# Norm, routing, plan and shared gate and up in one stage, and branch products on rounded halves, in a 3-layer float32 program

## What is computed

```python
# first block: three branches, each 512 wide, weighted by gates
proj = jnp.einsum('btnm,nmd->btnd', branches, w_branch[l])
gates = jax.nn.sigmoid(cols['merge']).reshape(b, t, N_BRANCH, D_MODEL)
x = x + (gates * proj).sum(axis=2) @ w_out[l]
...
# second block, each of 2 layers: two branches, then norm, modulation, experts
y = jax.nn.sigmoid(gate_a) * (o_a @ w_branch_a) + jax.nn.sigmoid(gate_b) * (o_b @ w_branch_b)
return y @ w_out
...
x = layer_norm(ALPHA * x + gate1 * y, ln1_g[l], ln1_b[l])
h = x * (1 + scale2) + shift2
y = moe_ffn(h, ...)
...
# moe_ffn: 64 experts in 8 groups; 4 groups, then 8 experts a token
scores = jax.nn.sigmoid((xt @ router_w).astype(jnp.float32))
...
shared = (jax.nn.silu(xt @ ws_gate) * (xt @ ws_up)) @ ws_down
return (routed + shared).reshape(B, S, D)
```

## Time and profile before

| | us |
|---|---|
| median of 3 runs | 3909.67 |
| lowest and highest | 3906.97, 3912.04 |
| the profiled execution | 3907.32 |
| its span, first to last instruction | 3905.2 |
| TensorE busy | 3391.9 (87%) |
| VectorE busy | 1570.4 (40%) |
| ScalarE busy | 942.6 (24%) |

### The profile page before, as it was taken

How to read it: one execution, slowest core, us unless ns; L and a number is a source line. 1 busy time by engine, 2 the same in 40 slices (tenths; PEclk the granted TensorE clock), 3 DMA queues, 4 the chain that set the end, 5 groups by cost and what they waited for, 6 DMA issues and landing times. The chain is left out here.

```text
span 3905.2 us, 47770 instructions
## 1 busy us (share of the span) xinstructions
PE 3391.9 (87%) x14923; PEld 2112.4 (54%) x14924; DVE 1570.4 (40%) x3950; ACT 942.6 (24%) x1993; POOL 200.1 (5%) x204
## 2 busy tenths in 40 slices
PE   3887887997999888997799999958899779999985
...
GB/s 122 79 21 28 44 79 39 177 143 140 134 195 134 93 137 23 70 39 54 285 407 400 406 395 402 369 175 129 23 68 41 54 282 415 402 400 392 391 289 194
DMA packets 287126, 748.55 MB, mean 192 GB/s; under 512 B 25883, under 2 KB 167581, under 8 KB 230788
## 3 DMA queue, kind: packets, MB, share of 16 engines
...
...
## 5 line engine op out<-in xcount | busy, mean ns | idle before, releaser
L2502 PE MATMUL up_ps<-experts,x_turned 128*64 128x512 f32 (+1 forms) x2256 | 699.0, 623 | 22.7 <-DMA experts<-in_w_up_dram 21.2
L2502 PEld LDWEIGHTS up_ps<-experts,x_turned 128*64 128x64 f32 (+1 forms) x2256 | 261.4, 161 | 383.2 <-issue 382.6
L257 DVE TENSOR_TENSOR pieces_lo<-weights,pieces_hi 128x512 fp32r<-128x512 f32 (+1 forms) x412 | 274.1, 682 | 314.4 <-ACT pieces_hi L251 313.1
L251 ACT CAST pieces_hi<-weights 128x512 fp32r<-128x512 f32 (+1 forms) x412 | 244.8, 613 | 452.9 <-PE banks L269 93.5
L2526 PE MATMUL y_ps<-experts,hid_turned 128*64 128x512 f32 (+1 forms) x1128 | 345.6, 601 | 1.6 <-ACT hid_turned L2583 1.6
L2661 DVE TENSOR_TENSOR hid_seats<-up_ps,gated 128x256 f32<-128x256 f32 x94 | 57.5, 612 | 607.4 <-ACT gated L2576 607.4
L267 PE MATMUL gate_ps<-h_hi,pieces_hi 128*128 128x512 f32 x624 | 262.4, 420 | 37.8 <-DVE pieces_lo L257 32.0
L267 PE MATMUL products<-h_hi,pieces_hi 128*128 128x512 f32 x464 | 195.4, 421 | 65.5 <-DVE pieces_lo L257 65.5
L269 PE MATMUL gate_ps<-h_hi,pieces_lo 128*128 128x512 f32 x624 | 247.0, 396 | 0.0
L268 PE MATMUL gate_ps<-h_lo,pieces_hi 128*128 128x512 f32 x624 | 246.8, 396 | 0.0
L2526 PEld LDWEIGHTS y_ps<-experts,hid_turned 128*64 128x64 f32 (+1 forms) x1128 | 117.5, 154 | 222.2 <-issue 222.2
...
## 6 DMA issues: line engine op xcount, KB each, us to landing
...
```

Source lines behind the costliest of these rows:

```text
L251: act.copy(self.like(view, self.hi[:, i % self.BUFFERS, :, :]), view).then_inc(s["hi_ready"], 1)
L257: dve.tensor_tensor(lo, view, hi.bitcast(F32), ALU.subtract).then_inc(s["lo_ready"], 1)
L2502: made = pe.matmul(up_ps[part, b, :].rearrange("p (h n) -> p h n", h=2), xT[:, b, k, part], experts.up(b + i)[:, :, k, :], start=(k == 0), ...
```

## The change

1. **Merges.** The branch outputs are rounded and split too, into the two halves' buffers that y uses later and a new pair for the last branch, and the branch product is made like the others, as a third piece of its unit (12 instructions in place of 4 in float32). Units now go branch by branch, the column tiles inside; the sums of all 8 tiles are kept where the first branches' outputs were. A chunk holds one unit, and VectorE frees it when it has split the third piece; the waits for `branch_made` go. The first block's ring has 3 slots of 32 x 128 columns instead of 36 x 128.
2. **One stage, `route_tokens`,** in place of the norm, modulation, transposes, `route` and `make_lists`. The norm works in rows: x is transposed to rows of tokens, VectorE takes mean and variance of each row, ScalarE normalises while it empties the bank, and the tiles are transposed back, where ScalarE applies gain and shift times ALPHA. The modulation makes h, from which rows of tokens are made for the gathers after the router's product. The shared gate and up products have their own weights buffer and stand around the counts and the plan. SyncE loads the first experts' weights (`first_loads`) as soon as the plan stands, still in this stage.
3. **The shared down product** moves into `routed_experts`, between the first searches for seats and the first turn; ScalarE copies its banks to `acc` first.
4. **Tables.** The gather table (40 + 640 columns in place of 1320) and the rotation table are loaded in every layer, and TensorE waits only for the gather table. The zeros are set by GpSimd in each layer.

The core of the diff:

```diff
-    for m in range(DK):
-        add("merge", *[w[:, :, C_MERGE + b * D + m * P:C_MERGE + b * D + (m + 1) * P] for b in range(3)],
-            *[rows(wb[b], 4)[:, :, m * P:(m + 1) * P] for b in range(3)])
+    for b in range(3):
+        for m in range(DK):
+            add("merge", w[:, :, C_MERGE + b * D + m * P:C_MERGE + b * D + (m + 1) * P],
+                rows(wb[b], 4)[:, :, m * P:(m + 1) * P])
...
         pieces = []
         for i in range(n):
-            c = c0 + i // n_branch
-            wm = ring.slot(c, DK, P, i % n_branch * DK * P)
-            pieces += [(c, wm[:, 0:4, :], False), (c, wm[:, 4:8, :], False)]
+            wm = ring.slot(c0 + i, DK, P)
+            pieces += [(c0 + i, wm[:, 0:4, :], False), (c0 + i, wm[:, 4:8, :], False),
+                       (c0 + i, ring.slot(c0 + i, 4, P, DK * P), True)]
...
                 for i in range(n):
-                    m, b = i // n_branch, i % n_branch
-                    wb = ring.slot(c0 + m, 4, P, n_branch * DK * P + b * 4 * P)
...
                         pe.wait_ge(s["gate_ready"], i - 1)
-                    split.product(pe, s, 2 * i, gate_ps[:, i % 2, :], h_hi, h_lo, 0, True, False)
-                    split.product(pe, s, 2 * i + 1, gate_ps[:, i % 2, :], h_hi, h_lo, 4, False, True)
-                    if b == 0:
-                        ring.wait(pe, c0 + m)
+                    split.product(pe, s, 3 * i, gate_ps[:, i % 2, :], h_hi, h_lo, 0, True, False)
+                    split.product(pe, s, 3 * i + 1, gate_ps[:, i % 2, :], h_hi, h_lo, 4, False, True)
                     if i >= 2:
                         pe.wait_ge(s["part_ready"], i - 1)
-                    for k in range(4):
-                        last = pe.matmul(branch_ps[:, i % 2, :], wb[:, k, :], oT[:, b, k, :], start=(k == 0),
-                                         stop=(k == 3))
-                    last.then_inc(s["branch_made"], 1)
-                    if b == n_branch - 1:
-                        pe.wait_ge(s["branch_made"], i + 1)
-                        pe.sem_inc(ring.used, 1)
+                    if m == 0:
+                        pe.wait_ge(s["o_split"], 4 * (b + 1))
+                    split.product(pe, s, 3 * i + 2, branch_ps[:, i % 2, :], o_hi[b], o_lo[b], 0,
+                                  True, True)
...
+                def round_branch(b, k):
+                    act.copy(o_hi[b][:, k, :], oT[:, b, k, :]).then_inc(s["o_rounded"], 1)
...
+                    if i == 0:
+                        for k in range(4):
+                            round_branch(0, k)
+                    if i in (1, 2):
+                        for k in (2 * i - 2, 2 * i - 1):
+                            round_branch(1, k)
+                    if DK + 2 <= i <= DK + 5 and i < last_unit:
+                        round_branch(2, i - DK - 2)
+                    split.round(act, s, 3 * i + 2)
+                    if i >= last_unit + 2:
+                        round_y(i - last_unit - 2)
...
+                def rest_of_branch(b, k):
+                    dve.wait_ge(s["o_rounded"], 4 * b + k + 1)
+                    dve.tensor_tensor(o_lo[b][:, k, :], oT[:, b, k, :], o_hi[b][:, k, :].bitcast(F32),
+                                      ALU.subtract).then_inc(s["o_split"], 1)
...
+        add("merge", w[:, :, C2_GA + m * P:C2_GA + (m + 1) * P],
+            (by_pair[0][:, :, m * P:(m + 1) * P], by_pair[1][:, :, m * P:(m + 1) * P]))
+    for m in range(DK):
+        add("merge", w[:, :, C2_GB + m * P:C2_GB + (m + 1) * P], wbb[:, :, m * P:(m + 1) * P])
...
+    def first_loads(self, sp, plan):
+        es = [sp.value_load(plan[0:1, at:at + 1], min_val=0, max_val=EXPERTS - 1) for at in (0, P, P + 1)]
+        for slot in range(3):
+            self.load_up(sp, slot, es[slot])
+        self.load_down(sp, self.WHOLE, es[0])
...
+                sp.dma_start(prog.gather[:, :], d["cst_norm"][:, 0:SELECT_2]).then_inc(s["gather_loaded"], 16)
+                sp.dma_start(rope[:, :], d["cst_rope"]).then_inc(s["rope_loaded"], 16)
+                for i, name in enumerate(("sgu_ln_g_2", "sgu_ln_b_2")):
+                    sp.dma_start(affine[:, i, :], d[name][l:l + 1, :].to_broadcast([P, SGU])).then_inc(s["affine_loaded"], 16)
...
                     if i == 3:
-                        if tables:
-                            pe.wait_ge(s["tables"], 16 * len(tables))
+                        pe.wait_ge(s["gather_loaded"], 16)
...
+                for j in range(2):
+                    sp.dma_start(shared_up[:, j, :, :], rows(experts.shared[j])).then_inc(s["shared_loaded"], 16)
+                sp.dma_start(shared[:, :, :], rows(experts.shared[2], 2)).then_inc(experts.shared_loaded, 16)
+                sp.wait_ge(s["h_copied"], 2 * TT)
                 sp.dma_start(d["tokens"].rearrange("(t p) n -> p t n", p=P), h_tok[:, :, :]).then_inc(s["stored"], 16)
+                sp.wait_ge(s["plan_ready"], 1)
+                experts.first_loads(sp, plan)
...
+                def forward(t):
+                    if t >= 2:
+                        pe.wait_ge(s["normalised"], 2 * (t - 1))
+                    for m in range(DK):
+                        last = pe.transpose(banks[:, t % 2 * 2 + m // 4, (m % 4) * P:(m % 4 + 1) * P],
+                                            xT[:, m, t * P:(t + 1) * P], prog.ident[:, :])
+                    last.then_inc(s["rows_turned"], 1)
...
+                def turn_h(i):
+                    t, j = i // 2, i % 2
+                    if i < 2:
+                        pe.wait_ge(s["x_made"], DK)
+                    else:
+                        pe.wait_ge(s["h_copied"], i - 1)
...
+                for t in range(TT):
+                    forward(t)
+                for k in range(DK):
+                    back(k)
                 for t in range(TT):
                     for k in range(DK):
+                        if t == 0:
+                            pe.wait_ge(s["h_made"], k + 1)
                         last = pe.matmul(bank[:, t, :], hT[:, k, t * P:(t + 1) * P], rw[:, k, :], start=(k == 0),
                                          stop=(k == DK - 1))
                 last.then_inc(s["made"], 1)
-                pe.wait_ge(experts.shared_loaded, 48)
-                for m in range(2):
-                    for j, (shared_ps, ready) in enumerate(((gate_ps, s["gate_made"]), (up_ps, s["up_made"]))):
-                        w = experts.up(experts.WHOLE)[:, j, :, :]
-                        for k in range(DK):
-                            last = pe.matmul(shared_ps[:, m, :], w[:, k, m * P:(m + 1) * P], hT[:, k, :],
-                                             start=(k == 0), stop=(k == DK - 1))
-                        last.then_inc(ready, 1)
+                for i in range(2 * TT):
+                    turn_h(i)
+                pe.wait_ge(s["shared_loaded"], 32)
+                shared_product(0, 0)
+                pe.wait_ge(s["chosen"], 1)
+                for t in range(TT):
+                    last = pe.matmul(count_ps, prog.ones[:, :], sel[:, t, :], start=(t == 0), stop=(t == TT - 1))
+                last.then_inc(s["counted"], 1)
+                for t in range(TT):
+                    for j in range(t + 1):
+                        last = pe.matmul(place_ps[:, t, :], before if j == t else prog.ones[:, :], sel[:, j, :],
+                                         start=(j == 0), stop=(j == t))
+                last.then_inc(s["counted"], 1)
+                shared_product(1, 0)
+                shared_product(0, 1)
+                pe.wait_ge(s["cols_ready"], 1)
+                pe.wait_ge(s["h_copied"], 2 * TT)
+                for i in range(4):
+                    last = pe.matmul(plan_ps[:, i, :], wide[:, i, :], prog.ident[:, :], start=True, stop=True)
+                last.then_inc(s["plan_turned"], 1)
+                shared_product(1, 1)
...
+                for t in range(TT):
+                    act.wait_ge(s["moments_ready"], t + 1)
+                    act.activation(root[:, t:t + 1], moments[:, t, 1:2], ACT.Sqrt,
+                                   bias=prog.ln_eps[:, 0:1]).then_inc(s["root_ready"], 1)
+                    act.wait_ge(s["offset_ready"], t + 1)
+                    for side in range(2):
+                        act.activation(rows_hat[:, t, side * 512:(side + 1) * 512], banks[:, t % 2 * 2 + side, :],
+                                       ACT.Identity, bias=rstd[:, t, 1:2], scale=rstd[:, t, 0:1]).then_inc(s["normalised"], 1)
+                act.wait_ge(s["folded"], 2)
+                for k in range(DK):
+                    act.wait_ge(s["back_made"], k + 1)
+                    act.activation(xT[:, k, :], turned[:, k % 2, :], ACT.Identity, bias=shift[:, k:k + 1],
+                                   scale=gain[:, k:k + 1]).then_inc(s["x_made"], 1)
...
+                row_stats(0)
+                row_stats(1)
+                row_scale(0)
+                row_stats(2)
+                row_scale(1)
```

(19 more changed lines are left out.)

303 lines of the change are left out of this document (156 added, 147 removed).

## The result

The changed kernel takes 3796.69 us (median of 4 runs, lowest 3790.24), the kernel before beside it 3910.86 (3906.97 to 3914.47). The ratio is 0.9703, with an interval of 0.9684 to 0.9722: 3.0% faster. I had said 3810, between 3788 and 3840. The profiled execution is the fastest of its runs, 3790.24 us with a span of 3788.4, so the span is 116.8 us shorter, where my sum had 98.

A forecast was written before the change was run, and what follows sets the result against it. TensorE was the engine to follow, busy 87%, full beside DMA in expert passes, gapless in merges, mostly waiting ahead of the experts. 45 + 45 + 8 = 98 us off 3907.3 gives 3809.3, said as 3810, between 3788 and 3840.

The forecast's parts named there:

- Merges: The 56 merge units: branch product in 12 instructions saves 41.4 us, drain waits 5.8, tails cost 2; sum 45 us.
- The wait of the next product for the branch product to drain (5.8 us over 19 waits): In the merges: this wait has no place in the new program, so its 5.8 us are saved.
- The tails of 2 us: At each merge's end one more tile of y is split after the last product: 0.7 us, 2 us in all.
- the upper bound: Merges: 49 us if all of the gain comes and the tails cost nothing.
- The three-buffer argument: Merges: pieces are written in time for TensorE, so the added splitting costs nothing; rival of late pieces, chance 0.06, 3855.
- Loads are the same bytes in smaller chunks: Merge weight loads: same bytes, three or four units of lead (25 us or more); no cost in the sum.
- The rival on supply: Merge weights landing too slowly would pace TensorE; gain gone at 34.8 us a chunk, 3959 at 38; chance 0.03.
- The stretch ahead of the experts: Out projection's end to first expert up product: 28.9 us earlier, 6.4 back for the moved product; 22.5 a layer, 45.
- Tables: Small table loads in both layers: less waiting and low clock in layer 0, 2.5 us more in layer 1; 7 to 8 less.
- The low clock ahead of the experts: Rival, chance 0.15: TensorE's clock stays low in the new stage; 12 us a layer, 24 in all, 3834.
- The early loads: First routed experts' weights asked for some 40 us earlier, costed at nothing; rival that passes gain, chance 0.08, 3800.
- the likeliest one: The whole kernel's likeliest case: 3810 us, with 3790 to 3830 of its own; chance 0.68.

The follow-up runs named there:

- e2: Changed kernel with the branch product in float32 on whole tiles, without the split of branch weights and outputs; 3845.49 us, ratio 0.9816.
- e1: Changed kernel with the merges, their lists of chunks and the ring of 36 x 128 columns of the kernel before; 3857.57 us, ratio 0.9847.
- e11: Changed kernel as it is, run again for comparison; 3795.76 us, ratio 0.9689.
- e7: Changed kernel without the shared expert's down product and the copies of its banks; 3783.74 us, ratio 0.9673.
- e8: Changed kernel with four bank pairs, counts at once, reordered shared products, half the shared down product under the lists, gather table behind first chunk; 3764.76 us, ratio 0.9620.
- e10: Changed kernel with ten products that nobody reads set into TensorE's three waits in the rows phase; 3798.06 us, ratio 0.9693.
- e3: Changed kernel with the first weights of experts asked for at the start of the experts' stage; 3795.44 us, ratio 0.9691.

## Why the prediction was right, and where it was short

- **Merges, 45 forecast, 53.5 measured.** The mechanism held, and the largest term: 41.4 us forecast for the product, 40.6 measured (e2). What was mis-sized is the step "The wait of the next product for the branch product to drain (5.8 us over 19 waits)": I took the idle time that the group lists as the price. By the spacing of the units, which the same trace had, it is 0.57 us behind each of the 19 and 0.4 behind two more, 11.6 us in all. The tails of 2 us did not come: from the last branch product to the out projection it takes as long in e2 as before. The last 1.3 us is TensorE's clock in the first unit (e2). The 53.5 also lies above the 49 that I gave as the upper bound, and my own terms without tails make 47.2, not 49. The three-buffer argument (no late piece) and "this work costs nothing" held: waits for pieces stayed at 31.9 us, units came at 8.16 us (9.12 where the sum of modulation rows stands between them).
- **"Loads are the same bytes in smaller chunks"** priced the loads by bytes and lead. It missed that each transfer occupies SyncE's queue, and that a stage ends only when the queue is through: 3.8 us at the end of a stage in the first block, which e1 gives back. In the table these 3.8 us are part of the piece up to the first merge, whose scatter between executions is larger. The rival on supply (34.8 us a chunk) did not come near: no chunk was late.
- **The stretch ahead of the experts, 22.5 a layer forecast, 25.0 measured.** The counts came at 49.0 us for 49.2 and the lists, with the two products of the hidden tile, at 80.8 for 81.9. On the way errors cancelled: normalised rows came 1.0 us later (19.5 for 18.5) and h 3.0 later (28.7 for 25.7), since these activations take 0.77 and 0.78 us and not 0.72 and the transposes ran at the low clock; the router did not pay the 2 us of clock, and the copies of h took 0.91 us each and not 1.04. That the counts came within 0.2 us of the forecast is luck to that extent. Of the 2.5 us above the forecast, 1.1 are in the lists, and 1.1 in the moved product, which paid 1.8 us of cold start where I had 2.9. Another execution of the changed kernel (e11) has the first up product at 153.49 and 154.43 us for 153.97 and 153.72, so half a microsecond of it is scatter. e7 puts the net price of the moved product at 8.3 and 7.9 us, 6.9 by my terms.
- **Tables, 7 to 8 forecast, 6.4 measured:** 10.1 less in layer 0 (9.3 forecast) and 3.7 more in layer 1 (2.5 forecast). The two parts of the forecast make 6.8, and 8 went into the sum. The table took 16.4 us to land though it is half the size: what stands ahead of it in the queue sets that rather than its size, since behind one chunk instead of four it landed in 6.0 (e8).
- **Rivals.** The low clock ahead of the experts was there (0.61 in the rows phase, 0.50 at the first searches), but not where its price was put: from the router to the plan the clock was 1.00. In the rows phase it costs 1 to 2 us a layer (e10), and 1.8 more in the moved product, not 12. What my low chance rested on held, the router's product at full clock: 7.33 us before, 7.41 now. The clock had come up ahead of it, in the turning back (0.50 in its first 3 us, 0.61 in the next 4). The Trainium skill (TensorE: Matmul & The Clock Gate, HAM oscillation) describes the bursts; by that, the trace agrees for the rows phase and for the first searches behind the wait at the stage's end, and not for the stretch between. The early loads gave nothing that e3 could take back, and no piece was late.
- The time lies 13 us under the likeliest one and still in that case's own range, 3790 to 3830. The two costs that were missed, the drain and the queue, have one sign: both were costs of before that no row lists as idle time at their full size.

The small rows of the table are TensorE's clock. The 0.8 us in each out projection is the number of its first products that run at the low level, 0.43 us apart and not 0.227: 11 and 12 before, 8 and 8 now. It is 6 to 14 in the other executions, whose out projections are the same code and take 47.0 to 48.6 us, so this is scatter. The 1.1 us in the first block stands in the sum of squares behind the out projection, 10.19 us before and 10.02 in e1, 9.09 in the changed kernel. Still open is whether the old merges bring that about: both executions that have them show it and none of the other eleven does (7.5 to 9.1 us), but nothing was tried on it alone.
